# A third Strassen block in ten gate/up pairs of a decoder layer, with sums of weights held in DRAM and silu on ScalarE

## What is computed

```python
def swiglu(h, w_gate, w_up, w_down):
    return (jax.nn.silu(h @ w_gate) * (h @ w_up)) @ w_down

# D_MODEL = 2048, D_FF = 5632
h = rmsnorm(x, norm_ffn_g[l])
x = x + swiglu(h, w_ffn_gate[l], w_ffn_up[l], w_ffn_down[l])
```

## Time and profile before

| | |
|---|---|
| median of 3 runs | 1742.57 (1742.5 to 1742.66) |
| the profiled execution | 1742.88, its span 1740.6 |
| PE busy | 1729.1 (99%), 7881 matmuls recorded |
| PE weight loads busy | 1435.1 (82%) |
| VectorE busy | 1379.7 (79%) |
| ScalarE busy | 1002.8 (58%) |
| GpSimd busy | 29.8 (2%) |
| DMA | 338.24 MB, mean 194 GB/s; 59.5% of the 16 engines on SyncE's queue |

### The profile page before, as it was taken

How to read it: one execution, slowest core, us unless ns; L and a number is a source line. 1 busy time by engine, 2 the same in 40 slices (tenths; PEclk the granted TensorE clock), 3 DMA queues, 4 the chain that set the end, 5 groups by cost and what they waited for, 6 DMA issues and landing times.

```text
span 1740.6 us, 20479 instructions
## 1 busy us (share of the span) xinstructions
PE 1729.1 (99%) x7881; PEld 1435.1 (82%) x7881; DVE 1379.7 (79%) x1521; ACT 1002.8 (58%) x1248; POOL 29.8 (2%) x54
## 2 busy tenths in 40 slices
PE   9999999999999999999999999999999999999998
PEld 7888888888888888888888888888888888888886
DVE  7577677887888787888665589888888878888887
ACT  6767678554656565555465465555555545555554
POOL 1100000000000000000000000000000000000000
PEclk9999999999999999999999999999999999999999
DMA  9565665666566655556755456566666566566663
GB/s 339 175 201 163 216 183 161 200 213 199 183 193 196 194 179 183 178 169 220 266 183 192 149 156 202 185 194 195 195 200 218 192 209 197 179 195 196 212 194 118
DMA packets 176049, 338.24 MB, mean 194 GB/s; under 512 B 10704, under 2 KB 15312, under 8 KB 175696
## 3 DMA queue, kind: packets, MB, share of 16 engines
q1 hardware_dynamic: 173376, 327.98, 59.5%
q0 software_dynamic: 1296, 5.24, 1.0%
q10 hardware_dynamic: 1280, 3.71, 0.5%
HBM read 334.80 MB, written 2.10 MB: 194 GB/s over the span
## 4 chain that ended last, share of the span: by engine, by line
PE 98%; DVE 1%; ACT 0%; DMA 0%; issue 0%; ACTq 0%; POOLq 0%; POOL 0%; DVEq 0%
PE group L492 28%; PE group L494 28%; PE group L493 28%; PE side L492 3%; PE side L494 3%; PE side L493 3%; PE side L555 2%; PE side L662 0%; PE side L697 0%; DMA x_T_in<-in_x_T 0%; DVE w_lo L1284 0%; PE side L627 0%; PE side L626 0%; PE side L625 0%; DVE x_res L1639 0%
## 5 line engine op out<-in xcount | busy, mean ns | idle before, releaser
L876 ACT ACTIVATE w_hi<-w_raw 128x1024 fp32r<-128x1024 f32 x612 | 615.0, 1019 | 446.6 <-PE group L494 431.1
L1284 DVE TENSOR_TENSOR w_lo<-w_raw,w_hi 128x1024 fp32r<-128x1024 f32 x612 | 702.8, 1172 | 167.6 <-ACT w_hi L876 159.9
L492 PE MATMUL group<-w_hi,x_hi 128*128 128x512 f32 x1412 | 554.3, 393 | 0.8 <-DVE w_lo L1352 0.6
L494 PE MATMUL group<-w_hi,x_lo 128*128 128x512 f32 x1412 | 549.9, 389 | 0.0
L493 PE MATMUL group<-w_lo,x_hi 128*128 128x512 f32 x1412 | 549.5, 389 | 0.0
L492 PEld LDWEIGHTS group<-w_hi,x_hi 128*128 128x128 f32 x1412 | 265.1, 188 | 57.3 <-DVE w_lo L1284 2.6
L494 PEld LDWEIGHTS group<-w_hi,x_lo 128*128 128x128 f32 x1412 | 265.1, 188 | 55.6
L493 PEld LDWEIGHTS group<-w_lo,x_hi 128*128 128x128 f32 x1412 | 265.2, 188 | 53.4
L876 ACT ACTIVATE w_hi<-w_sums 128x1024 fp32r<-128x1024 f32 x114 | 121.1, 1062 | 210.1 <-PE group L494 173.7
L1284 DVE TENSOR_TENSOR w_lo<-w_sums,w_hi 128x1024 fp32r<-128x1024 f32 x114 | 139.4, 1224 | 97.1 <-ACT w_hi L876 97.1
L492 PE MATMUL group<-w_hi,inner_hi 128*128 128x512 f32 x274 | 107.0, 391 | 0.2 <-DVE x_res L1639 0.2
(11 more groups left out here) (336 smaller groups left out, 1897.4 us busy)
## 6 DMA issues: line engine op xcount, KB each, us to landing
w_raw<-in_w_in SPq DMA_DIRECT2D x223, 512.0 KB, 4.3
w_raw<-in_w_ffn_gate SPq DMA_DIRECT2D x88, 512.0 KB, 4.1
w_raw<-in_w_ffn_up SPq DMA_DIRECT2D x88, 512.0 KB, 4.6
w_raw<-in_w_ffn_down SPq DMA_DIRECT2D x88, 512.0 KB, 4.8
w_raw<-in_w_rnn_proj SPq DMA_DIRECT2D x32, 512.0 KB, 4.7
w_raw<-in_w_attn_proj SPq DMA_DIRECT2D x32, 512.0 KB, 4.7
w_raw<-in_w_mix_out SPq DMA_DIRECT2D x32, 512.0 KB, 4.8
w_raw<-in_w_xkv SPq DMA_DIRECT2D x16, 512.0 KB, 3.7
```

The lines of the kernel that those rows point to most:

```text
L492: nc.tensor.matmul(out, h, whi[:, s, k, :], start=start, stop=False)
L494: return nc.tensor.matmul(out, l, whi[:, s, k, :], start=False, stop=stop)
L876: nc.scalar.activation(whi[:, s, ks], src[:, ks], ACT.Copy).then_inc(hi_ready[s], 1)
L1284: V_.tensor_tensor(wlo[:, s, ks], src[:, ks], whi[:, s, ks].bitcast(F32), ALU.subtract).then_inc(w_ready[s], 1)
```

## The change

The plan of ten gate/up pairs (all but (a, 0)) gets a third Strassen block, W1, and another order; the pair has 22 steps: the blocks at steps 4 to 7, 10 to 13 and 16 to 19, O7 at steps 20 and 21. (a, 0) keeps its plan, but its sums of activations now cover three blocks.

The sums C and D of W1's weights are not made in the pair. In ten earlier stretches (RG-LRU stages, `mix`, `mem_k`, `mem_q`) ScalarE loads the gate and up weights of W1 (two DMAs of 512 KB), VectorE sums them in three operations, and ScalarE stores the sums to an internal DRAM tensor (1 MB). In the pair SyncE loads C and D of W1 like other chunks. Silu is now one function on ScalarE (`ACT.Silu`) instead of tanh and an operation on VectorE; `halve` is gone.

```diff
-UP_PLAN = "O0 O1 W3 O2 O4 W5 O6 O7".split()
+UP_PLAN = "O0 O2 W1 O4 W3 O6 W5 O7".split()
...
+AHEAD_OF = [(("gate_a", _j), 1) for _j in range(1, FA)] + [(("gate_b", _j), 1) for _j in range(FB)]
+AHEAD_EARLY = 5
+AHEAD_LOAD = [("xr", 0, 6), ("g_rnn", 1, 2), ("xr", 1, 6), ("g_rnn", 2, 2), ("xr", 2, 6),
+              ("mix", 0, 5), ("mix", 1, 6), ("mix", 2, 6), ("mix", 3, 6), ("mem_q", 0, 1)]
+AHEAD_SUM = [("yr", 0, (2, 4, 5)), ("xr", 1, (2, 3, 4)), ("yr", 1, (2, 4, 5)), ("xr", 2, (2, 3, 4)), ("yr", 2, (2, 4, 5)),
+             ("mix", 1, (1, 2, 4)), ("mix", 2, (1, 2, 4)), ("mix", 3, (1, 2, 4)), ("mem_k", 0, (5, 6, 7)), ("mem_q", 0, (4, 5, 6))]
+AHEAD_STORE = [("g_rnn", 1, 2), ("xr", 1, 6), ("g_rnn", 2, 2), ("xr", 2, 6), ("g_rnn", 3, 2),
+               ("mix", 1, 6), ("mix", 2, 6), ("mix", 3, 6), ("mem_q", 0, 1), ("mem_v", 0, 0)]
...
+            def load_sums(n):
+
+                s, _ = raw_of(n)
+                b, which = AHEAD[n]
+                earlier, used = slot_of(LOADED[LOAD_OF[n] - RR])
+                sync.wait_ge(sem("ahead_moved"), 48 * len(AHEAD_OF))
+                sync.wait_ge(w_ready[earlier], START + used + 1)
+                sync.dma_start(raw[:, s], held_sums[b, :, which]).then_inc(raw_full[s], 16)
...
+            def ahead_load(b):
+
+                if b > 0:
+                    act.wait_ge(sem("ahead_summed"), b)
+                for half, w in enumerate(ahead_weights(b)):
+                    act.dma_start(ahead_raw[b // AHEAD_EARLY][:, half * CK:(half + 1) * CK, :], w).then_inc(sem("ahead_moved"), 16)
+
+            def ahead_store(b):
+
+                act.wait_ge(sem("ahead_summed"), b + 1)
+                act.dma_start(held_sums[b], ahead_sums[b // AHEAD_EARLY][:, :, :, :]).then_inc(sem("ahead_moved"), 16)
...
-            def gate_tanh(first):
+            def gate_silu(first):
 
                 wait_taken(act, GI[first])
                 for tt in range(TT):
-                    last = nc.scalar.activation(silu[:, tt, :], fold[:, 0, tt, :], ACT.Tanh, scale=hrstd["x2"][:, tt:tt + 1])
-                last.then_inc(sem("tanh"), 1)
+                    last = nc.scalar.activation(silu[:, tt, :], fold[:, 0, tt, :], ACT.Silu, scale=rstd["x2"][:, tt:tt + 1])
+                last.then_inc(sem("silu"), 1)
...
-                        if KIND.get(m) == "A":
+                        if KIND.get(m) == "A" and m + 2 not in AHEAD:
                             weight_sums(m)
...
+            def ahead_sum(stage, j, c):
+
+                for b, (of, group, steps) in enumerate(AHEAD_SUM):
+                    if (of, group) != (stage, j) or c not in steps:
+                        continue
+                    t, sums = ahead_raw[b // AHEAD_EARLY], ahead_sums[b // AHEAD_EARLY]
+                    if c == steps[0]:
+                        dve.wait_ge(sem("ahead_moved"), 48 * b + 32)
+                        then(V_.tensor_tensor(sums[:, :, 0, :], t[:, 0:4:3, :], t[:, 2:3, :].to_broadcast([P, 2, GW]), ALU.add))
+                    if c == steps[1]:
+                        then(V_.tensor_tensor(sums[:, 1, 1, :], sums[:, 0, 0, :], t[:, 3, :], ALU.add))
+                    if c == steps[2]:
+                        V_.tensor_tensor(sums[:, 0, 1, :], sums[:, 1, 1, :], t[:, 1, :], ALU.add).then_inc(sem("ahead_summed"), 1)
...
-            def gate_silu():
+            def inner_tok(second):
 
                 made[0] += 1
-                dve.wait_ge(sem("tanh"), made[0])
-                marks["silu"] = marked(V_.scalar_tensor_tensor(silu[:, :, :], silu[:, :, :], 1.0, fold[:, 0], ALU.add, ALU.mult))
-
-            def inner_tok():
-
-                dve.wait_ge(sem("vector_chain"), marks["silu"])
+                dve.wait_ge(sem("silu"), made[0])
+                wait_taken(dve, GI[second])
...
                             if c == 3:
                                 gained_lo(side[1], 3, xhi, xlo, KG - 1, "x2")
                                 variance("x2")
-                                halve("x2")
+                                dve.wait_ge(sem("rstd_x2"), 1)
```

More of the change, by code:

```diff
@@ L137 @@
 END["g_rnn", 0] = len(OPENING) - 1
-LOADED = [_n for _n in range(CHUNKS) if KIND.get(_n) not in ("C", "D")]
+AHEAD_OF = [(("gate_a", _j), 1) for _j in range(1, FA)] + [(("gate_b", _j), 1) for _j in range(FB)]
[6 more added lines that the diff above has]
+               ("mix", 1, 6), ("mix", 2, 6), ("mix", 3, 6), ("mem_q", 0, 1), ("mem_v", 0, 0)]
+AHEAD = {}
+for _b, (_first, _kp) in enumerate(AHEAD_OF):
+    for _c, (_kind, _of, _half) in enumerate(STEPS[_first]):
+        if _of == _kp and _kind in "CD":
+            AHEAD[N0[_first] + _c] = (_b, "CD".index(_kind))
+LOADED = [_n for _n in range(CHUNKS) if KIND.get(_n) not in ("C", "D") or _n in AHEAD]
 LOAD_OF = {_n: _load for _load, _n in enumerate(LOADED)}
-SUMMED = {_kind: sorted(_n for _n in KIND if KIND[_n] == _kind) for _kind in "CD"}
+SUMMED = {_kind: sorted(_n for _n in KIND if KIND[_n] == _kind and _n not in AHEAD) for _kind in "CD"}
 SUM_OF = {_n: _w + 1 for _kind in "CD" for _w, _n in enumerate(SUMMED[_kind])}
@@ L254, in build, with ahead_weights @@
         w_sums = at("w_sums", LW, [2, CK, GW])
+        ahead_raw = [at("ahead_raw0", S, [2 * CK, GW]), at("ahead_raw1", STAGE[0], [2 * CK, GW])]
+        ahead_sums = [at("ahead_sums0", S + 8 * K1, [2, CK, GW]), w_sums]
+        held_sums = nc.dram_tensor("held_sums", (len(AHEAD_OF), P, 2, CK, GW), F32, kind="Internal").ap()
+        def ahead_weights(b):
+            (name, j), kp = AHEAD_OF[b]
+            rows, col = slice(kp * CK * P, (kp + 1) * CK * P), (j + (FA if name == "gate_b" else 0)) * GW
+            return [dram[w][rows, col:col + GW].rearrange("(k p) n -> p k n", p=P) for w in ("w_ffn_gate", "w_ffn_up")]
         PAD = region(4 * NB * (4 + SEQ))
@@ L284, in build @@
         mem_parts = new("mem_parts", [TT, 2])
-        silu_scale = new("silu_scale", [TT])
         smax, nmax = new("smax", [TT, NB]), new("nmax", [TT, NB])
@@ L350, in pair @@
                 for c, (_, kp, half) in enumerate(STEPS[first]):
+                    n = N0[first] + c
                     if half is not None:
-                        load(N0[first] + c, ws[half], row0 + kp * CK * P, cols[half])
+                        load(n, ws[half], row0 + kp * CK * P, cols[half])
+                    elif n in AHEAD:
+                        load_sums(n)
             def x_pair(c):
@@ L808, in _ @@
                     first = ("gate_" + part, j)
-                    for c, kind, kp in pair_of(first, xhi, xlo, xs_hi, xs_lo, X_SUMS):
+                    for c, kind, kp in pair_of(first, xhi, xlo, us_hi, us_lo, X_SUMS):
                         if c == 2 and (part, j) == ("a", 0):
@@ L876, in splits, with ahead_moves @@
                         nc.scalar.activation(whi[:, s, ks], src[:, ks], ACT.Copy).then_inc(hi_ready[s], 1)
+            def ahead_load(b):
[6 more added lines that the diff above has]
+                act.dma_start(held_sums[b], ahead_sums[b // AHEAD_EARLY][:, :, :, :]).then_inc(sem("ahead_moved"), 16)
+            def ahead_moves(stage, j, c):
+                for b, at_ in enumerate(AHEAD_STORE):
+                    if at_ == (stage, j, c):
+                        ahead_store(b)
+                for b, at_ in enumerate(AHEAD_LOAD):
+                    if at_ == (stage, j, c):
+                        ahead_load(b)
             def evac(g, end, dst, scale, func):
@@ L993, in _ @@
                 for c in splits(N0["g_rnn", j], CG):
+                    ahead_moves("g_rnn", j, c)
                     if j == 0:
@@ L1149, in _ @@
                 for c in splits(N0["mix", j], CG):
+                    ahead_moves("mix", j, c)
                     if j == 0 and c in (2, 3):
@@ L1460, in _ @@
                 for c in splits(N0["g_rnn", j], CG):
+                    ahead_sum("g_rnn", j, c)
                     if j > 0:
@@ L1663, in _ @@
                 for c in splits(N0["mix", j], CG):
+                    ahead_sum("mix", j, c)
                     if j == 0 and c in (0, 1):
@@ L1775, in _ @@
                         if c == 0 and q == 0:
-                            gate_silu()
-                            inner_tok()
+                            inner_tok(("up_" + part, groups - 1))
                         if c == 3 and q == 0:
```

43 lines of the change are left out of this document (27 added, 16 removed).

## The result

The changed kernel takes **1756.33 us** (median of four runs, 1755.56 to 1756.44) against 1742.62 of the kernel before on the same chip: a ratio of **1.0077**, 95% interval 1.0060 to 1.0095. It is slower by 13.7 us; forecast were 12.6 us and 1755.2. The profiled execution took 1756.24, its span 1754.0, 13.4 more than before.

The account below looks back on a forecast made before the run. PE was taken as the bound: matmuls times their spacing, plus waits. -6.8 + 12.2 + 5.3 + 1.6 + 0.3 = +12.6 us gave 1755.2 us, range for 8 in 10 1748 to 1761.

Parts of the forecast that it names:

- Step 1: Ten gate/up pairs: a third block replaces an ordinary pair of chunks, 30 matmuls fewer, -6.8 us.
- Step 2: End of ten pairs: join stands behind a split and four folds, PE waits 1.22 us each, +12.2 us.
- Step 3: Middle of seven pairs: W3's sums follow the inner sums, PE waits 0.75 us at step 10, +5.3 us.
- Step 4: First gate/up pair: activation sums for three blocks instead of two delay the split of its step 7, +1.6 us.
- Step 5: Silu on ScalarE costs what Tanh did; VectorE's 1.23 us less per pair brings no time, 0.
- Step 6: Sums made ahead in earlier stages: nearly all in VectorE's idle time, some 0.1 us in each `yr` group, together +0.3.
- 7 raw loads: Ten pairs: 20 more loads of 512 KB are issued early enough, 0.
- A: Rival for the ten pairs: the matmuls are saved in full, 1736 us, chance 8%.
- B: Rival: the join at pair ends is not late, the middle of the pairs is, 1743.0 us, chance 8%.
- C: Rival: the join at pair ends is late, the middle of the pairs is not, 1749.9 us, chance 7%.
- D: Rival: chunks held in DRAM come late in the pairs, slower still, 1765 at 1 us beyond, chance 5%.

Follow-up runs that it names:

- experiment 1: Changed kernel with the four folds and the first half's join one step earlier at the end of the ten pairs: 1745.47 us.
- experiment 2: Kernel before with only the last block of the ten pairs moved, one ordinary pair of chunks behind it instead of two: 1756.84 us.
- experiment 3: Changed kernel with the inner sums at steps 9, 10 and 11 instead of 4, 5 and 6 of seven pairs: 1749.57 us.
- experiment 6: Kernel before with Silu on ScalarE alone, VectorE's operation and the halvings gone: 1742.09 us against 1742.55.
- experiment 5: Changed kernel with the first pair's activation sums for two of three blocks made one group earlier: 1755.61 us.
- experiment 9: Kernel of experiment 8 with VectorE's addition ahead of `x_lo` in the last `cross_out` group: 1736.68 us.
- experiment 8: Changed kernel with folds and join earlier, join before fourth fold, inner sums later, two blocks' activation sums earlier, `yr` sums ahead at later steps: 1736.04 us.
- experiment 7: Kernel of experiment 1 with the first half's join also moved ahead of the fourth fold operation: 1743.45 us.
- experiment 4: Changed kernel with nothing made ahead; W1's C and D chunks read straight from the gate and up weights: 1756.11 us.
- experiment 10: Kernel of experiment 9 with two more ordinary chunks ahead of the first block of the first `down` pair: 1735.89 us.

## Why the prediction was right, step by step

| step | forecast | measured | from |
|---|---|---|---|
| 1 matmuls | -6.8 | -6.8 | (b, 0), without waits at either end: 42.16 to 41.48, 0.68 x 10 |
| 2 late join | 10 x 1.22 = 12.2 | 10 x 1.36 = 13.6 | PE's starts, experiments 1 and 2 |
| 3 W3's sums | 7 x 0.75 = 5.3 | 7 x 0.73 = 5.1 | PE's starts, experiment 3 |
| 4 first pair | +1.6 | +1.6 | 43.11 to 44.72 |
| 5 Silu | 0 | -0.3 | step 8 of (a, 2), experiment 6 |
| 6 sums ahead | +0.3 | +0.5 | three `yr` groups, 0.17 each |
| 7 raw loads | 0 | 0 | no wait of PE for a load in these pairs |
| sum | +12.6 | +13.7; the spans differ by 13.4 | |

Most of the 0.3 by which the parts exceed the spans are small gains that no step had, 0.1 in each of two `down` pairs. The forecast was 1.1 us too low: step 2 by 1.4, and the errors of the other steps, 0.3 or less each, take 0.3 of it back.

**Step 1.** The Trainium skill's figure ("TensorE: Matmul & The Clock Gate", Back-to-back issue gap, 215.8 ns for 512 columns) would make it 0.65 a block, an estimate. The two undisturbed pairs show 42.16 - 41.48 = 0.68, the 0.2267 of the rows; the trace doesn't agree with the page. The page's other figure, 131 ns sustained, is further off still.

**Step 2 was right in mechanism and 0.14 too small.** The chain split, folds, join was counted to end 6.50 behind O7's first matmul. It ends at 6.59 (O7 starts 5.44 before 1201.62, at 1196.18; the join ends at 1202.77), since there are a few hundredths more between the operations. The remaining 0.05 is PE's: behind a wait the second matmul starts 0.33 after the first, as before, but the next seven are 0.233 apart and not 0.2267 (1203.16 to 1204.79). The "end + 0.16" holds also for a wait of over 1 us, and some 0.05 have to be added.

**Step 3 was right**: the split for step 10 ends at 1181.04 and PE starts 0.05 later. The three pairs without inner sums show no wait there. From first matmul to first matmul (a, 1) and (b, 1) last 43.6 and 43.7, the seven 44.7, where the forecast had 43.6 and 44.6. (b, 0) lasts 42.7: it has no transposes, which the forecast overlooked in these lengths, not in the sum.

**Step 4 has the right sum and incomplete working.** The waits add up to 1.6, but the first is for `x_lo` at step 6 (0.8), which the longer sums delay too; I had looked only at step 7's split. The sum comes out even so: PE goes on at step 8 only when that step's split has ended, and what it has waited at step 6 it doesn't wait again at steps 7 and 8. Experiments 5 and 9 then showed that I took the cause too narrowly: not a piece of work at the wrong step, but a stretch of 20 us in which VectorE has little time to spare, with a wait for GpSimd's root in it that nothing needs there.

**Step 5 was 0.3 too high**: VectorE's 1.23 us do stand ahead of something PE waits for, in (a, 2), which the forecast had at nothing.

**Step 6 was too small** by 0.2. The earlier trace rows answer to 68.17 + 1.22 = 69.39 here, 1.36 later than before and not 1.18; 0.11 of it is the whole program's later start, by PE's transposes of this group (54.95 against 54.84). PE's turn came at 69.33 + 0.11 = 69.44, so `conv_lo` was 0.05 ahead of it, and still each group lost 0.17. A lead that small counts as none.

```profile
68.17 1.22 DVE L1575 TENSOR_TENSOR conv_lo<-conv_T,conv_hi 128x1024 fp32r<-128x1024 f32 x1
```

**Rivals.** A (all of the gain kept) would have needed what experiment 8 does, and 1736 was its time. B (the join is not late) and C (the middle is not late) fall, since both waits are there. Their times, 1743.0 and 1749.9, are those of experiments 7 and 3 (1743.45 and 1749.57), which take the one wait away and leave the other. D falls by experiment 4 and by W1's undisturbed chunks; the loads from the held tensor land in 4.9, like the others.

## What to carry to other kernels

Count not only the work that a plan saves but where its tail stands: whatever frees a buffer (join, addition) should have, in its engine's program, nothing ahead of it that the buffer doesn't need, and that was worth 13 us here against the 6.8 of the saved matmuls. Before work is moved forward, ask what idle time lies between its new place and the wait: only that is gained, and the next hand-over behind the new place becomes the late one (experiments 5, 9 and 10). Read PE's losses from its starts and the chain, not from its busy share, which was 99% with and without 13 us of waits.
